# Hybrid mLSTM and sliding-window attention layer: four decode-state slots with early loads, and prompt scores in 64-row contractions

## What is computed

```python
def mlstm_step(...):                                # per chunk
    w = exp(dmat - m_row); w_int = exp(inter - m_row)
    num = w_int * (q @ C) + (q @ k.T * w) @ v        # n is carried as a 257th column of C
    h = num / max(|den|, exp(-m_row))
    C_new = decay * C + (wk * k).T @ v               # n_new alike

def sink_attend(q, k, v, mask, sinks):               # 16 query heads of 64, 4 key heads, window 128
    s = where(mask, q @ k.T * 64 ** -0.5, -inf)
    mx = max(max(s), sink); p = exp(s - mx)
    return (p / (sum(p) + exp(sink - mx))) @ v

merged = sigmoid(ga) * branch_a + sigmoid(gb) * branch_b
x = x + merged @ w_out
x = x + square(relu(rmsnorm(x) @ w_up)) @ w_down
```

## Time and profile before

| | us |
|---|---|
| median of 3 runs (1845.96 to 1847.26) | 1846.01 |
| span of the profiled execution | 1838.2 |
| TensorE busy | 1774.4 (97%) |
| VectorE busy | 809.4 (44%) |
| ScalarE busy | 523.1 (28%) |
| GpSimd busy | 72.4 (4%) |
| mean granted TensorE clock | 0.982 of 2.4 GHz |

### The profile page before, as it was taken

One profiled execution on the slowest core, in us unless ns is written; L12 is line 12 of the kernel. 1 busy time (PEld: TensorE's weight loads), 2 busy tenths in 40 slices (PEclk: granted clock), 3 DMA queues, 4 the chain that ended last, 5 costly groups with the idle time before them and its releaser, 6 DMA issues.

```text
span 1838.2 us, 26328 instructions
## 1 busy us (share of the span) xinstructions
PE 1774.4 (97%) x10443; PEld 1622.1 (88%) x10443; DVE 809.4 (44%) x1769; ACT 523.1 (28%) x1191; POOL 72.4 (4%) x149
## 2 busy tenths in 40 slices
PE   7999977998999999999999999999999999999998
PEld 7999956996899888888999998888888889999996
DVE  5313212342115544466452544444444544444447
ACT  5424311331224533345330331211121222222222
POOL 3001110110100000000000100000000000000001
PEclk9999986998899999999999999999999999999999
DMA  6131125212512112311133011111111111111112
GB/s 199 48 90 43 45 60 94 41 35 73 72 29 41 24 32 50 67 24 24 24 93 109 24 47 47 46 46 46 46 46 40 30 44 46 46 46 46 46 58 97
DMA packets 140605, 99.26 MB, mean 54 GB/s; under 512 B 82328, under 2 KB 132512, under 8 KB 140520
## 3 DMA queue, kind: packets, MB, share of 16 engines
q1 hardware_dynamic: 140520, 98.08, 20.6%
HBM read 88.43 MB, written 11.60 MB: 54 GB/s over the span
## 4 chain that ended last, share of the span: by engine, by line
PE 85%; DMA 5%; SPq 1%; DVE 1%; ACT 0%; issue 0%; POOL 0%; POOLq 0%; ACTq 0%; DVEq 0%
PE bank L725 25%; PE bank L1077 21%; PE bank L1050 21%; PE bank L1036 6%; DMA out<-Cin 4%; PE bank L865 3%; PE bank L687 3%; PE bank L897 2%; PE bank L782 1%; PE bank L790 1%; PE bank L808 1%; PE bank L819 1%; PE bank L785 1%; DMA bc<-gate_rows 1%; DMA Cin<-in_state_n 0%; PE bank L765 0%
## 5 line engine op out<-in xcount | busy, mean ns | idle before, releaser
L1891 DVE TENSOR_TENSOR x<-bank,x 128x512 f32<-128x512 f32 x288 | 195.5, 689 | 139.2 <-PE bank L1077 137.5
L1050 PE MATMUL bank<-xT_hi,w_hi 128*128 128x384 f32 (+1 forms) x768 | 250.5, 326 | 1.0 <-DVE xT_lo L1513 1.0
L1050 PE MATMUL bank<-xT_hi,w_lo 128*128 128x384 f32 (+1 forms) x768 | 250.4, 326 | 0.0
L1050 PE MATMUL bank<-xT_lo,w_hi 128*128 128x384 f32 (+1 forms) x768 | 250.3, 326 | 0.0
L1077 PE MATMUL bank<-w_hi,hid_hi 128*128 128x512 f32 x576 | 227.1, 394 | 0.0
L1077 PE MATMUL bank<-w_lo,hid_hi 128*128 128x512 f32 x576 | 226.1, 392 | 0.0
L1077 PE MATMUL bank<-w_hi,hid_lo 128*128 128x512 f32 x512 | 204.1, 399 | 0.0
L725 PE MATMUL bank<-xT_hi,w_hi 128*128 128x384 f32 (+1 forms) x1008 | 197.7, 338 | 3.5 <-ACT w_hi L1124 3.5
L725 PE MATMUL bank<-xT_lo,w_hi 128*128 128x384 f32 (+1 forms) x1008 | 189.6, 330 | 0.0
L725 PE MATMUL bank<-xT_hi,w_lo 128*128 128x384 f32 (+1 forms) x1008 | 186.5, 326 | 0.0
L1448 ACT ACTIVATE relu<-bank 128x384 f32<-128x384 f32 (+1 forms) x96 | 45.4, 473 | 493.8 <-PE bank L1050 493.8
(11 more groups left out here) (204 smaller groups left out, 2330.8 us busy)
## 6 DMA issues: line engine op xcount, KB each, us to landing
raw<-in_w_in SPq DMA_DIRECT2D x64, 256.0 KB, 4.4
raw<-in_w_up SPq DMA_DIRECT2D x16, 1024.0 KB, 5.5
raw<-in_w_down SPq DMA_DIRECT2D x16, 1024.0 KB, 4.9
raw<-in_w_in SPq DMA_DIRECT2D x10, 1024.0 KB, 5.9
xin<-in_x_prompt SPq DMA_DIRECT2D x8, 512.0 KB, 4.0
Cin<-in_state_C SPq DMA_DIRECT2D x8, 512.0 KB, 4.4
bc<-gate_rows SPq DMA_DIRECT2D x32, 128.0 KB, 4.2
out<-Cin SPq DMA_DIRECT2D x8, 512.0 KB, 6.2
```

The source lines that it names most:

```text
L1050: last = nc.tensor.matmul(bank[n % 4][:, 0:cn], w[:, slot, k * WCOLS + tile * P:k * WCOLS + (tile + 1) * P], x[:, k, c0:c0 + cn], start=(s ...
L1891: nc.vector.tensor_tensor(v, bank[4 + d % 4][:, :], v, ALU.add).then_inc(free_v, 1)
```

## The change

`Cin` gets four slots, one for each (hh, half) of a pass, with a semaphore each. All four loads of a pass are issued after the broadcast of block 4. The broadcasts for blocks 0 and 1 of the second pass are issued around the stores of the first two slots. The wait for the stores moves from ScalarE and GpSimd to TensorE, ahead of attention.

Keys are held as `akT`, both heads of a pair in one slab of 128 rows. A unit of prompt attention is now two query heads (gp) of both key heads: products over 64 rows, the two key heads by turns, each into its own bank. Probability slots, sinks and `pT` follow that order, and the value products take the two halves by turns. The zeroing of `akz` and half of ScalarE's copies into it fall away, and the key output is transposed directly.

```diff
-                Cin = a2("Cin", [P, 2, 4, VA])
...
+                Cin = a2("Cin", [P, 4, 4, VA])
...
-            akz = a("akz", [P, NKV, T])
+            akT = a("akT", [P, 2, T])
...
             def load_cin(n):
                 p, hh, half = n // 4, n // 2 % 2, n % 2
                 h = 2 * p + hh
-                if n >= 2:
-                    sp.wait_ge(cin_out, 32 * 4 * p if n % 4 < 2 else 32 * (n - 1))
...
+                if p:
+                    sp.wait_ge(cin_out, 32 * 4)
+                sp.dma_start(Cin[:, n % 4, :, 0:DV],
...
             def mlstm(p):
                 s0 = p * S_PER
                 if p == 0:
                     sp.wait_ge(gate_nat, 1)
-                load_cin(4 * p)
-                load_cin(4 * p + 1)
-                load_bc(s0)
-                load_bc(s0 + 1)
+                    load_bc(s0)
+                    load_bc(s0 + 1)
                 fill(FILL_ML[p][0])
                 for i in range(2, NT):
                     fill(FILL_ML[p][2 * i - 3])
                     fill(FILL_ML[p][2 * i - 2])
                     load_bc(s0 + i)
+                    if i == CIN_AT:
+                        for n in range(4 * p, 4 * p + 4):
+                            load_cin(n)
...
                 fill(FILL_ML[p][2 * NT - 1])
+                if p == 0:
+                    load_bc(S_PER)
                 for n in range(4 * p, 4 * p + 2):
                     store_cin(n)
-                    load_cin(n + 2)
                 fill(FILL_ML[p][2 * NT])
+                if p == 0:
+                    load_bc(S_PER + 1)
                 for n in range(4 * p + 2, 4 * p + 4):
                     store_cin(n)
...
             def at_scores(u):
-                i, p, half = at_unit(u)
-                kv = 2 * p + half
+                i, p, gp = at_unit(u)
...
-                for g in range(GRP):
-                    out = bank[3 + g // 2][:, (g % 2) * 256 + lo:(g % 2) * 256 + 256]
-                    last = nc.tensor.matmul(out, aqT[:, p * GRP + g, cols(i)],
-                                            akz[:, kv, (i - 1) * P + lo:(i + 1) * P], start=True, stop=True)
+                for gg in range(2):
+                    for half in range(2):
+                        at = slice(64 * half, 64 * half + 64)
+                        last = nc.tensor.matmul(bank[3 + half][:, gg * 256 + lo:gg * 256 + 256],
+                                                aqT[at, p * GRP + 2 * gp + gg, cols(i)],
+                                                akT[at, p, (i - 1) * P + lo:(i + 1) * P], start=True, stop=True)
...
             def at_values(pair):
...
-                for half in range(2):
-                    u, kv = 2 * pair + half, 2 * p + half
-                    for kb in range(2):
-                        if kb:
-                            pe.wait_ge(at_p1, u + 1)
-                        elif i:
-                            pe.wait_ge(at_p0, prev_count(u))
+                for kb in range(2):
+                    if kb:
+                        pe.wait_ge(at_p1, 2 * pair + 2)
+                    elif i:
+                        pe.wait_ge(at_p0, prev_count(2 * pair + 1))
+                    for half in range(2):
+                        kv = 2 * p + half
...
                 for x, i in enumerate((NT - 2, NT - 1)):
-                    for kv in range(NKV):
-                        p, half = divmod(kv, 2)
-                        last = nc.tensor.matmul(bank[5 + x][0:rows_of(i), p * P:(p + 1) * P], akz[:, kv, cols(i)],
-                                                ident[:, :], start=(half == 0), stop=(half == 1))
+                    for p in range(2):
+                        last = tr(bank[5 + x][0:rows_of(i), p * P:(p + 1) * P], akT[:, p, cols(i)], P)
...
+                pe.wait_ge(cin_out, 32 * 8)
                 prompt(0, FILL_P0)
...
-                        act.wait_ge(cin_out, 32 * 8)
...
-                    for half in range(2):
-                        at = slice(64 * half, 64 * half + 64)
-                        ins = nc.scalar.activation(akz[at, 2 * tile + half, c0:c0 + cn], src[at, 0:cn], ACT.Copy)
-                    ins.then_inc(free_a, 1)
+                    nc.scalar.activation(akT[:, tile, c0:c0 + cn], src[:, 0:cn], ACT.Copy).then_inc(free_a, 1)
...
-                nc.scalar.activation(pT[:, u % 2, 0, :], bank[5][:, :], ACT.Copy).then_inc(at_p0, 1)
+                nc.scalar.activation(pT[:, :, 0, gp * 256:gp * 256 + 256], by_half(bank[5][:, :]), ACT.Copy)\
+                    .then_inc(at_p0, 1)
...
-                nc.vector.tensor_copy(pT[:, u % 2, 1, :], bank[6][:, :]).then_inc(at_p1, 1)
+                nc.vector.tensor_copy(pT[:, :, 1, gp * 256:gp * 256 + 256], by_half(bank[6][:, :])).then_inc(at_p1, 1)
...
-            pool.wait_ge(cin_out, 32 * 8)
             pool.wait_ge(pc_out, 64)
...
-            for kv in range(NKV):
-                link(nc.gpsimd.memset(akz[64 * (1 - kv % 2):64 * (1 - kv % 2) + 64, kv, :], 0.0))
```

More of the change, by code:

```diff
@@ L338, in layer_kernel @@
         ml_cl = sem("ml_cl")
-        cin_in = [sem(f"cin_in{n}") for n in range(2)]
+        cin_in = [sem(f"cin_in{n}") for n in range(4)]
         cin_out = sem("cin_out")
@@ L425, in layer_kernel @@
         S_PER = NT
+        CIN_AT = 4
         AQ_BLOCKS = (12, 14)
@@ L435, in at_unit, with by_half, sinks_of, slots_of @@
             return u % (2 * NB) // 2, u // (2 * NB), u % 2
+        def by_half(v):
+            return v.rearrange("p (h c) -> p h c", h=2)
+        def sinks_of(p, gp):
+            return sink_b[:, :].rearrange("p (k a b) -> p k a b", a=2, b=2)[:, 2 * p:2 * p + 2, gp, :]
+        def slots_of(v):
+            return v.rearrange("p (h b) -> p h b", h=2)
         def prev_count(u):
@@ L532, in load_cin @@
                 h = 2 * p + hh
-                if n >= 2:
-                    sp.wait_ge(cin_out, 32 * 4 * p if n % 4 < 2 else 32 * (n - 1))
-                sp.dma_start(Cin[:, half, :, 0:DV],
-                             state_C[0, 4 * half:4 * half + 4, h].rearrange("b k v -> k b v")).then_inc(cin_in[half], 16)
-                sp.dma_start(Cin[:, half, :, DV:VA],
+                if p:
+                    sp.wait_ge(cin_out, 32 * 4)
+                sp.dma_start(Cin[:, n % 4, :, 0:DV],
+                             state_C[0, 4 * half:4 * half + 4, h].rearrange("b k v -> k b v")).then_inc(cin_in[n % 4], 16)
+                sp.dma_start(Cin[:, n % 4, :, DV:VA],
                              state_n[0, 4 * half:4 * half + 4, h].rearrange("b k -> k b").unsqueeze(2),
-                             allow_slow_non_contiguous=True).then_inc(cin_in[half], 16)
+                             allow_slow_non_contiguous=True).then_inc(cin_in[n % 4], 16)
             def store_cin(n):
@@ L545, in store_cin @@
                 sp.dma_start(s_C[0, 4 * half:4 * half + 4, h].rearrange("b k v -> k b v"),
-                             Cin[:, half, :, 0:DV]).then_inc(cin_out, 16)
+                             Cin[:, n % 4, :, 0:DV]).then_inc(cin_out, 16)
                 sp.dma_start(s_n[0, 4 * half:4 * half + 4, h].rearrange("b k -> k b").unsqueeze(2),
-                             Cin[:, half, :, DV:VA], allow_slow_non_contiguous=True).then_inc(cin_out, 16)
+                             Cin[:, n % 4, :, DV:VA], allow_slow_non_contiguous=True).then_inc(cin_out, 16)
             def mlstm(p):
@@ L805, in ml_sampled @@
                 for half in range(2):
-                    pe.wait_ge(cin_in[half], 32 * (2 * p + hh + 1))
+                    pe.wait_ge(cin_in[2 * hh + half], 32 * (p + 1))
                     for b in range(4 * half, 4 * half + 4):
                         last = nc.tensor.matmul(bank[6 + hh][0:n, 0:VA], qz[:, hh, 64 * b:64 * b + 64],
-                                                Cin[:, half, b % 4, :], start=False, stop=(b == NSEQ - 1))
+                                                Cin[:, 2 * hh + half, b % 4, :], start=False, stop=(b == NSEQ - 1))
                 if hh == 1:
@@ L920, in ss_scores @@
                     nc.tensor.matmul(out[:, 0:P], q, kcT[at, b % 2, p, :], start=True, stop=True)
-                    last = nc.tensor.matmul(out[:, P:192], q, akz[at, kv, SEQ:T], start=True, stop=True)
+                    last = nc.tensor.matmul(out[:, P:192], q, akT[at, p, SEQ:T], start=True, stop=True)
                 last.then_inc(ss_s, 1)
@@ L1301, in at_prev @@
             def at_prev(u):
-                if at_unit(u)[0] == 0:
+                i, _, gp = at_unit(u)
+                if i == 0:
                     return
@@ L1693, in at_own @@
             def at_own(u):
+                gp = at_unit(u)[2]
                 dve.wait_ge(at_t, u + 1)
```

9 lines of the change are left out of this document (5 added, 4 removed).

## The result

The change takes the kernel from 1846.63 us (median of 4, 1845.96 to 1847.29) to **1781.87 us** (median of 4, 1778.77 to 1786.36): ratio 0.9647, 95% interval 0.963 to 0.9664. The prediction was 1786 us, with a range of 1772 to 1811. The profiled run of the changed kernel took 1778.77 us, with a span of 1777.0 us; all that follows is read from it. The four runs differ with the mean granted clock: 0.995, 0.992, 0.991 and 0.989 for 1778.77, 1780.95, 1782.79 and 1786.36 us.

The account below looks back on a forecast made before the run. TensorE, busy 97% of the span, was taken as the bound. Part one, mLSTM passes and projections start, 44.8 us, plus part two, prompt attention and key output, 15.1, took 59.9 off 1846.0: 1786 us, range 1772 to 1811.

Parts of the forecast that it names:

- State waits: Ends of both mLSTM passes: TensorE's 13.0 and 8.1 us waits for decode state loads go, 21.1 us saved.
- Broadcasts: Starts of the mLSTM passes: earlier broadcast rows remove waits of 9.9 and 0.5 us, 10.4 us saved together.
- Late gate block: Second mLSTM pass: first gate block's weight load, behind closely spaced stores, lands near 291 us, costing 1.5 us.
- Start of the attention projections: Before attention: an earlier mask saves 3.1 of the 3.5 us wait plus 1.5 of low clock, 4.6 us.
- Work at the lower clock: mLSTM work after removed waits runs at full clock, saving 12.0 us; clock falls at 64-row key products cost 1.8.
- Scores: Prompt attention: row halves overlap, 28 units save 0.86 us each, 24.1 us; shape changes cost 9.0; 128-column units gain nothing.
- New waits: Prompt attention: shorter scores make four units wait 0.25 us for their probabilities, costing 1.0 us.
- Value order: Prompt attention: interleaving the column halves of the value products saves nothing, as a group already takes 1.87 us.
- Row halves that don't overlap: Rival, prompt attention: score units stay at 1.73 us and pay shape changes, 1809 us; chance 0.17.
- Colliding transfers: Rival: stores and gate block load queue up, block 11 us late, mask saves nothing, 1802 us; chance 0.08.
- The clock in prompt attention: Rival: 64-row products lower the clock there; gain gone once 60 us run so, up to 2033 us; chance 0.02.
- From span to median: Whole kernel: the median of the runs lies 7.8 us over the profiled span, taken as unchanged by the change.

Follow-up runs that it names:

- experiment 4: Changed kernel with the second pass's first two broadcasts issued at that pass's start, behind the stores: 1789.93 us, ratio 0.9682.
- one head a unit: Changed kernel with each attention unit again four query heads of one key head, 64-row products in one row half: 1806.82 us, ratio 0.9783.
- slots alone: Kernel before with only the four state slots, early loads and earlier broadcasts; store waits stay on ScalarE and GpSimd: 1809.47 us, ratio 0.9793.
- old value order, experiment 3: Changed kernel with both value products of one column half again ahead of those of the other: 1788.55 us, ratio 0.9672.
- mask behind the blocks: Changed kernel with the mask's transfers put behind the weight block loads of the attention projections: 1782.30 us, ratio 0.9638.
- Experiment 1: Kernel before with each part of the change by itself: state slots, loads and broadcasts 1809.47 us; 64-row scores, unit order and key output 1830.55 us.
- experiment 6: Changed kernel with mask transfers and two state stores later, then wider products: 128 state columns 1778.47 us, 128 key rows 1769.78, both 1769.76.
- scores alone: Kernel before with only the 64-row scores, akT, new unit order and direct key output: 1830.55 us, ratio 0.9908.
- experiment 6's base: Changed kernel with mask transfers behind the projections' weight blocks and the first pass's last two state stores behind the gate block: 1777.57 us, ratio 0.9631.

## Why the prediction was right, and where it was not

*State waits, 21.1 us: right.* They are gone to the last tenth. The loads stand at 159.2 to 168.3 us and the last landed at 172.7; "before 180" holds, and nothing behind them is late.

*Broadcasts, 10.4 us: right.* The first step has no wait; the late broadcasts of experiment 4 bring back 12.5 us there and 8 in the median.

*Late gate block, 1.5 us: right in kind, and in size by luck.* The second step waits 3.96 us instead of 2.35, so 1.6; the block was put at "near 291" and landed at 291.81. But four other profiles have the same order of stores and gate block, and their second step waits 4.54 us (one head a unit), 4.87 (slots alone), 5.15 (old value order) and 6.47 (mask behind the blocks): 2.2 to 4.1 more than 2.35. The reason was only half read: the small stores hold the queue, not the large ones.

*Start of the attention projections, 4.6 us: wrong.* The failed step is "the mask can be made right after the last transposes, 9 us earlier ... I take only 3.1 of the 3.5 us". The working named the right objection, that the mask's store "joins the queue behind the last state stores", and then discounted it to 0.4 us. In the earlier trace rows GpSimd waited for those stores; now the mask's transfers do: from the last state store's issue (422.82) to the first weight load (445.80) are 22.98 us, and 23.1 before. The wait is 4.9 us instead of 0.4, with the clock low behind it (0.57 from 452 to 460 us). Experiment 1 takes it apart: with a fall of the clock ahead of it, as before, the wait is 2.2 to 2.7 us, so the early mask saves 1 to 2 us and not 3.1; the other 2 us or so of the 4.9 are there because TensorE comes to the same load that much sooner when its clock has not fallen.

*Work at the lower clock, 12.0 us less 1.8: too small.* The sum forgot 1.1 us of waits of the key products for VectorE: 0.53 twice where before had 0.41 once, and three more of 0.14. Added up, the waits behind 130 us went from 39.5 to 12.1 us: 27.4, where the working has 21.1 + 10.4 + 3.1 - 1.5 = 33.1. The remaining 16.6 of the head's 44.0 us are work that runs faster, where it has 12.0 + 1.5 - 1.8 = 11.7. So the 44.8 came out right by two errors of about 5 us that cancel: waits over-, clock underestimated. That is luck only in part, since some 2 us of the wait at the attention projections is time that the clock had given. Nor is the clock's share one number: experiment 1 has the same waits and 12 us more in the head. The step "I keep those two [falls] and add 0.6 of one" treated as a count what differs between kernels and runs. The products that bring these falls were named rightly, the 64-row key products, and experiment 6 shows it.

*Scores, 24.1 us less 9.0 of shape changes: right, and tested apart.* The overlap is worth 26.3 us, the shape changes cost 7.85. That units of 128 columns gain nothing was wrong: their eight instructions start within 0.44 us where they took some 0.8. The weight loads keep up with them too, and 4 x 0.4 us is most of the difference to 24.1. The row half was rightly read from the column halves.

*New waits, 1.0 us: right in kind, too small.* Six of 0.22 to 0.29 us are the ones foreseen; twice 0.78 us ahead of the last value group of a half were not. Together 3.0. *Key output, 1.0: 1.6 us* (the stage between the halves). So part two is 26.3 - 7.85 - 3.0 + 1.6 = 17.1. *Value order, nothing: right* (experiment 3). The rule that matmuls start in program order, from the Trainium skill (TensorE: Matmul & The Clock Gate, "What overlaps and what doesn't"), would by the working have made the old order slower; 1.87 us in both orders does not bear that out here.

*The rivals.* Row halves that don't overlap: refuted by 1.06 us a group. Colliding transfers: partly true, with 1.6 us at the gate block (up to 4.1 in other profiles) and most of the mask's saving lost, not 11. The clock in prompt attention: 1.00 throughout in the profile after, though its 64-row scores come in pairs. Of the eleven other profiles with 64-row scores, five have one fall at the start of the second half, behind a wait of 1.07 us (1.7 us lost); the two with full-row scores have none, which is too few to tell. The rival's 60 us are far off either way. The profiled spans differ by 61.2 us, where the working has 59.9.

*From span to median: "7.8 over the span, which I take as unchanged" was a wrong step.* In the profile after, and in that of the scores alone (1830.27 us for a span of 1828.5), device time lies 1.8 us over the span. The other 6.0 were no constant: by this offset the profiled run of before took some 1840.0 us, an estimate, and no timed run of before took under 1842.4. Experiment 1 shows in what kind of wait such runs differ. The profile after is a quick run as well, 3.1 us under its median. So in medians the change brings 64.8 us, 3.6 more than between the two profiles, and the working's 59.9 was taken from a kernel in a good run.

## What to carry to other kernels

When a wait is moved to let a transfer start earlier, ask what stands in the queue in front of it: if the wait was for the same stores, the transfer queues behind them and little is gained (1 to 2 us here); moving the needed load ahead is what counts. Before two waits are compared, look when the waiting engine came to them: one that comes sooner waits longer for the same load. Two contractions over half the rows, alternated between the row halves and banks, run side by side and pay for their changes of shape; half-row products that run alone for microseconds can bring falls of the clock (10.2 us lost in the head of experiment 6's base), and rows of zeros took them away with no time added to the products. Changes that remove waits near such a stretch should be timed together, since effects there did not add (37.7 and 16.6 us apart, 64.8 together).

## What was not expected of the hardware

- Key products over 64 rows, some 5 us at a time, were followed by falls of the granted clock from 2.4 to 1.2 GHz though TensorE was busy, in some runs and not in others (the profile after has none behind those at 245 and 395 us); over 128 rows with zeros in the upper 64 they were not, at the same 3.69 us for twelve. Products of 64 output columns left the clock alone when the rows were full.
- Two products in different row halves run side by side: eight 256-column instructions in 1.06 us instead of 1.83, in one row half alone 1.92.
- A store of 2 KB in 4-byte elements cost the queue more than one of 512 KB: without them the large stores landed in 2.9 us instead of 7.7 to 18.6, and a 1 MB load was issued in 2.9 us instead of 13.9.
- The effects of two independent parts missed their sum by 10.5 us in the medians, while the change's own runs spread over 7.6; in the profiles nearly all of it lies in the granted clock of a stage that only one of them touches. Why the slots alone see more of its falls than the whole change, with the same products on TensorE there, stays open; the profile with the mask behind the blocks, which has the whole change, shows falls at the same five places (249 to 430 us), so it is not a matter of the edit alone.
